# A Hymba encoder layer on Trainium2: every gate/up tile from 4 to 15 by seven block products, with the weight sums made by accumulating DMA

## The chip, the cores and the metric

The kernel runs on one core of a Trainium2 chip. The metric is the device time of one execution in microseconds. Before the change it is 1041.13 us, the median of 3 runs (1039.52 to 1042.09).

## The reference

One encoder layer over 16 meta tokens and 512 sequence tokens of width 1024. Its parts are a layer norm at the input, a SwiGLU network, a token mixer (windowed attention beside a gated linear attention), and a second SwiGLU network; a layer norm with a scaled residual follows each of the three. The change touches the first half of the two SwiGLU networks (f = 0 and f = 1):

```python
def swiglu(h, w_gate, w_up, w_down):
    return (jax.nn.silu(h @ w_gate) * (h @ w_up)) @ w_down
h = layer_norm(DN_ALPHA * h + 0.5 * swiglu(h, ffn1_w_gate, ffn1_w_up, ffn1_w_down), ffn1_ln_g, ffn1_ln_b)
```

Here h has 528 rows in the first network and 512 in the second (the meta tokens are dropped at the end), w_gate and w_up are 1024 x 2816, and w_down is 2816 x 1024. All inputs are float32.

## The kernel before

**Precision.** Each float32 operand is split into a high and a low half in f16, scaled by a power of two. A product then takes three matmuls: high by high, low by high, high by low. The scale of a weight chunk comes from a bound on its largest absolute value. ACT sums absolute values along each row (`weight_sum`, L1310) or DVE takes the row maximum (`chunk_max`, L1793); POOL reduces over the partitions (`over_all`, L2681); DVE makes the scale in four small instructions (`scale_of`, L1775 to L1780). Then ACT writes the high half (L1295, L1333 to L1336, L1344, L1349) and DVE the low half, in one SCALAR_TENSOR_TENSOR (L1815, L1873 to L1881, L1887, L1895).

**Tiles.** The 2816 hidden columns are 22 tiles of 128. Tile m needs 1024 x 128 columns of w_gate and of w_up: the weight chunk c = GU[f] + m, of 2048 float32 columns in 128 partitions (1024 KB), loaded by SP in two DMAs into one of two `stage` slots (L546, L547). SP loads chunk m as soon as the low half of chunk m - 2 is written (`w_ready`).

**Two ways to do a tile.** A plain tile takes 8 blocks of 128 rows for gate and 8 for up, three matmuls each, over all tokens: 96 matmuls of 264 columns in the first network, 48 of 512 in the second. A seven tile sees gate and up as a 2 x 2 block matrix (B11 and B21 the upper and lower half of gate, B12 and B22 those of up), and the tokens as a 2 x 2 one, and takes 7 block products in place of 8, as Strassen and Winograd do: 7 x 4 x 3 = 84 matmuls of 264 (256 in the second network) columns, `seven_product` (L682). It needs four sums of weight blocks, T1 to T4, and four sums of token blocks, S1 to S4 (made once for each network). DVE makes T1 to T4 in three instructions (`weight_sums`, L1860 to L1864), and combines the seven results with four additions (`product_sum`, L1908, L1912). Their order on PE is products 1, 6, 5, 7, then 2, 3, 4; products 2, 3 and 4 go on in banks that hold earlier products, so that product 2 waits until ACT has copied product 1 out (`p1_copy`, L1355), and products 3 and 4 wait for the second and third of DVE's additions (`seven_sum`).

**Order.** Before, tiles 4, 6, 8, 10, 12 and 14 are seven tiles and the tiles between them plain ones. PE does the first four products of tile m, the gate half of tile m + 1 (`gu_part`, L732), the last three products of tile m, and the up half of tile m + 1. Each engine's program is an order written out by hand in a loop over `SEVEN_AT`; semaphores tie them together. An engine that waits holds up all that stands behind it.

Of the kernel before, what the change touches and what calls it, by code (L numbers as in the profile page):

```python
# [24 lines left out]
F16 = mybir.dt.float16  # L25
# [93 lines left out]
B_STEPS = 9  # L119
# [6 lines left out]
def build(nc, x_in, meta_in, params, rel_in, head_in, ident_in, masks_in, reset_in, w2_in,  # L126
          gate, up, down, w_in, w_out, out):
    with ExitStack() as ctx:
# [132 lines left out]
        t_sum = part("arena", [P, 4, 4 * P])  # L261
        seven_w = part("arena", [P, 2 * N_PROD * 4 * P]).bitcast(F16).rearrange("p (b q i n) -> p b q i n", b=2, q=2, i=N_PROD)
# [137 lines left out]
        t_done = sem("t_done")  # L400
        seven_hi = sem("seven_hi")
        seven_ready = sem("seven_ready")
        gate_half_hi = sem("gate_half_hi")
        gate_half_ready = sem("gate_half_ready")
# [139 lines left out]
        def _(sp):  # L544
# [9 lines left out]

            for i in range(N_TOK):
                sp.dma_start(x_tok[:, i, :], x_in[i]).then_inc(x_loaded[i], 16)
                if i == 1:
                    load_gu(0, 0, 0)
            load_gu(0, 1, 1)
            for f in range(2):  # L560
                for m in range(2):
                    if f:
                        sp.wait_ge(w_ready, GU[f] + m - 1)
                        load_gu(f, m, (GU[f] + m) % 2)
                with sp.Fori(0, (N_GU - 2) // 2) as i:
                    for t in range(2):
                        sp.wait_ge(w_ready, GU[f] + 1 + t + 2 * i)
                        load_gu(f, 2 * i + 2 + t, (GU[f] + t) % 2)
# [18 lines left out]
        def _(pe):  # L587
# [99 lines left out]
            def seven_first(f, m):  # L687
                g = seven(f, m)
# [26 lines left out]

            def gu_part(f, m, g):
                s = m % 2
                if g == 0:
                    pe.wait_ge(gate_half_ready, seven(f, m - 1) + 1)

                    pe.wait_ge(hid_done, KF * f + m + 1)
                else:
                    pe.wait_ge(w_ready, GU[f] + m + 1)
                for k in range(KD):
                    for wp, xp in PRODUCTS:
                        w = wsp[:, (GU[f] + m) % 2, wp, (g * KD + k) * P:(g * KD + k + 1) * P]
                        for h in [None] if f else range(2):
                            if h is None:
                                dst, x = acc(1, 4 * s + 2 * g), tokens(1, xs[:, xp, k, :])
                            else:  # L730
                                dst, x = acc_half(f, 4 * s + 2 * g, h), xs[:, xp, k, token_half(2 * f, h)]
                            mm = nc.tensor.matmul(dst, w, x, start=k == 0 and wp + xp == 0, stop=k == KD - 1 and xp == 1)  # L732
                mm.then_inc(gu_ready if g else gate_part, 1)
# [50 lines left out]
            def ffn(f):  # L784
# [15 lines left out]
                for m in range(PAIR_END, KF):  # L800
# [410 lines left out]
        def _(act):  # L1211
# [112 lines left out]
            def seven_split_hi(f, m):  # L1324
                c, g = GU[f] + m, seven(f, m)
                slot = c % 2
                scale = wscale[:, slot:slot + 1]
                w = seven_w[:, g % 2, 0, :, :]
                quarter = stage[:, slot, 0:GU_COLS].rearrange("p (q n) -> p q n", n=4 * P)
                act.wait_ge(w_scale, 4 * c + 3)  # L1330
                if g >= 2:
                    act.wait_ge(seven_done, N_PROD * (g - 1))
                nc.scalar.activation(w[:, B11:B21 + 1, :], quarter[:, 0:2, :], ACT.Copy, scale=scale).then_inc(seven_hi, 1)  # L1333
                nc.scalar.activation(w[:, B22, :], quarter[:, 3, :], ACT.Copy, scale=scale).then_inc(w_hi, 1)
                act.wait_ge(t_done, 3 * g + 3)
# [1447 lines left out]
```

## Time and profile before

| what | value |
|---|---|
| median of 3 runs | 1041.13 us (1039.52 to 1042.09) |
| the profiled execution: its time, its span | 1039.09 us, 1037.3 us |
| granted TensorE clock, mean | 0.988 |
| busy: PE, PEld, DVE, ACT, POOL | 970.1, 693.6, 760.3, 494.8, 52.1 us |
| tiles 4 to 15, first network | 73.22 to 196.38 us of the span |
| tiles 4 to 15, second network | 717.52 to 838.22 us of the span |

Durations of instructions are from this one execution. Matmuls are pipelined: one shows some 276 ns, but a group's start to the next group's start, divided by its matmuls, gives the rate at which PE takes them. A busy PE that is idle nowhere is therefore read from starts.

### The profile page before, as it was taken

To read this page: it belongs to the slowest core of one execution; us is meant where nothing else is said; L and a number is where in the kernel's file an instruction comes from. 1 tells how busy PE (TensorE), PEld (TensorE's weight loads), DVE (VectorE), ACT (ScalarE), POOL (GpSimd) and SP (SyncE) were. 2 spreads that over 40 slices of the span, in tenths; PEclk is the share of its full clock that TensorE was granted. 3 is DMA by queue.
4 is the path that set the end of the run, shared out by engine and by line. 5 is a ranking of instruction groups with operands and counts; after the bars stand their busy time and mean duration, and the time that the engine had idled before them with its cause. 6 is when DMAs were issued, how large, how long until landed. Compare 5 with 4: busy or idle time off the path is not lost.

```text
span 1037.3 us, 17455 instructions
## 1 busy us (share of the span) xinstructions
PE 970.1 (94%) x7131; PEld 693.6 (67%) x7131; DVE 760.3 (73%) x1344; ACT 494.8 (48%) x707; POOL 52.1 (5%) x96
## 2 busy tenths in 40 slices
PE   2999999999999999999997899899899999999995
PEld 1888888888788886875565437665566644434584
DVE  6877766577987676877567978878777667889634
ACT  5576655244422245763335752567666434342214
POOL 0000000000020000000000010001000000011000
PEclk9999999999999999999998989999999999999999
DMA  5233322233334300212111012122332322424002
GB/s 210 84 111 122 114 91 94 77 109 120 112 119 152 123 2 1 82 42 71 52 41 42 1 35 88 49 74 82 123 122 88 117 82 82 163 99 170 15 1 82
DMA packets 24993, 89.26 MB, mean 86 GB/s; under 512 B 3035, under 2 KB 5427, under 8 KB 24915
## 3 DMA queue, kind: packets, MB, share of 16 engines
q1 hardware_dynamic: 23904, 87.17, 24.6%
q8 instruction: 56, 0.92, 0.4%
q10 hardware_dynamic: 1011, 0.99, 0.3%
q14 instruction: 22, 0.18, 0.1%
HBM read 86.05 MB, written 2.10 MB: 85 GB/s over the span
## 4 chain that ended last, share of the span: by engine, by line
PE 57%; DVE 25%; ACT 10%; issue 5%; DMA 2%; POOL 1%; SPq 0%; ACTq 0%; DVEq 0%
PE PS L732 9%; PE PS L682 9%; PE PS L758 8%; PE PS L853 7%; PE PS L652 6%; DVE cmax L1793 5%; PE PS L760 4%; DVE wsp L1815 4%; PE PS L763 3%; ACT wsp L1295 2%; PE PS L827 1%; DVE big L2020 1%; ACT H L1289 1%; PE PS L1133 1%; PE PS L976 1%
## 5 line engine op out<-in xcount | busy, mean ns | idle before, releaser
L652 PE MATMUL PS<-xs,wsp 128*128 128x264 f16 (+1 forms) x1344 | 195.4, 307 | 5.6 <-DVE wsp L1815 4.5
L652 PEld LDWEIGHTS PS<-xs,wsp 128*128 128x128 f16 x1344 | 131.0, 98 | 68.9 <-DVE wsp L1815 7.9
L732 PE MATMUL PS<-xs,wsp 128*128 128x264 f16 (+1 forms) x864 | 130.9, 310 | 0.0
L1793 DVE TENSOR_REDUCE cmax<-stage 128x1 f32<-128x2048 f32 (+2 forms) x47 | 120.2, 2557 | 4.5 <-DMA stage<-in_w_out 3.6
L1295 ACT ACTIVATE wsp<-stage,wscale 128x2048 f16<-128x2048 f32 (+2 forms) x34 | 70.8, 2081 | 100.0 <-DVE wscale L1779 78.1
L732 PEld LDWEIGHTS PS<-xs,wsp 128*128 128x128 f16 x864 | 84.5, 98 | 39.9
L2681 POOL PARTITION_ALL_REDUCE call<-cmax x73 | 48.8, 669 | 894.8 <-DVE cmax L1793 652.4
L1815 DVE SCALAR_TENSOR_TENSOR wsp<-stage,wscale,wsp 128x2048 f16<-128x2048 f32 (+2 forms) x34 | 83.3, 2449 | 12.8 <-ACT wsp L1295 12.8
L758 PE MATMUL PS<-big,arena 128*128 128x264 f16 (+1 forms) x792 | 89.4, 274 | 0.0
L758 PEld LDWEIGHTS PS<-big,arena 128*128 128x128 f16 x792 | 77.5, 98 | 11.5
L763 PE MATMUL PS<-big,wsp 128*128 128x264 f16 x660 | 75.1, 276 | 1.4 <-DVE big L2020 1.3
L760 PE MATMUL PS<-big,wsp 128*128 128x512 f16 x330 | 72.1, 379 | 2.5 <-DVE big L2020 1.7
L763 PEld LDWEIGHTS PS<-big,wsp 128*128 128x128 f16 x660 | 64.1, 98 | 12.2 <-issue 1.5
L682 PE MATMUL PS<-X,arena 128*128 128x264 f16 (+1 forms) x576 | 67.8, 274 | 0.0
L853 PE MATMUL PS<-xs,wsp 128*128 128x264 f16 (+1 forms) x384 | 67.3, 328 | 0.0
L682 PEld LDWEIGHTS PS<-X,arena 128*128 128x128 f16 x576 | 56.3, 98 | 7.5
L760 PEld LDWEIGHTS PS<-big,wsp 128*128 128x128 f16 x330 | 31.7, 98 | 42.9 <-issue 2.8
L682 PE MATMUL PS<-xs,arena 128*128 128x264 f16 (+1 forms) x432 | 53.7, 274 | 5.0 <-DVE big L1918 3.7
L853 PEld LDWEIGHTS PS<-xs,wsp 128*128 128x128 f16 x384 | 35.8, 98 | 24.2 <-issue 1.9
L682 PEld LDWEIGHTS PS<-xs,arena 128*128 128x128 f16 x432 | 42.0, 98 | 13.8 <-issue 6.3
L1310 ACT ACTIVATE big<-stage 128x2048 f16<-128x2048 f32 x26 | 49.3, 1897 | 2.8 <-DMA stage<-in_up 2.8
L1827 DVE SCALAR_TENSOR_TENSOR big<-PS,oscale,tmp_a 128x528 f32<-128x528 f32 (+1 forms) x32 | 24.2, 757 | 31.5 <-ACT tmp_a L1302 31.4
(267 smaller groups left out, 1421.8 us busy)
## 6 DMA issues: line engine op xcount, KB each, us to landing
stage<-in_gate SPq DMA_DIRECT2D x44, 512.0 KB, 3.7
stage<-in_up SPq DMA_DIRECT2D x44, 512.0 KB, 4.5
stage<-in_down SPq DMA_DIRECT2D x32, 704.0 KB, 5.3
stage<-in_w_in SPq DMA_DIRECT2D x16, 512.0 KB, 4.6
stage<-in_w_out SPq DMA_DIRECT2D x8, 512.0 KB, 4.2
X<-in_x SPq DMA_DIRECT2D x4, 512.0 KB, 6.2
out_T<-H SPq DMA_DIRECT2D x16, 128.0 KB, 1.7
stage<-in_w_in SPq DMA_DIRECT2D x2, 576.0 KB, 4.8
```

Source lines behind the costliest of these rows:

```text
L652: return nc.tensor.matmul(dst, w, x, start=k == 0 and wp + xp == 0, stop=k == KD - 1 and xp == 1)
L682: mm = nc.tensor.matmul(PS[:, 4 * (m % 2) + bank, 0:ln_width(2 * f)], seven_w[:, seven(f, m) % 2, wp, w, k * P:(k + 1) * P], seven_tokens( ...
L732: mm = nc.tensor.matmul(dst, w, x, start=k == 0 and wp + xp == 0, stop=k == KD - 1 and xp == 1)
L758: mm = nc.tensor.matmul(PS[:, bank, 0:ln_width(2 * f)], w, x[:, token_half(2 * f, h)], **flags)
L760: mm = nc.tensor.matmul(acc(1, bank), w, tokens(1, x), **flags)
L763: mm = nc.tensor.matmul(PS[:, bank + g, 0:HALF], w, x[:, token_half(0, g)], **flags)
L853: mm = nc.tensor.matmul(dst, x if lhs_is_x else w, w if lhs_is_x else x, start=k == 0 and wp + xp == 0, stop=k == KD - 1 and xp == 1)
L1295: nc.scalar.activation(wsp[:, slot, 0, 0:cols], stage[:, slot, 0:cols], ACT.Copy, scale=wscale[:, slot:slot + 1]).then_inc(w_hi, 1)
L1310: nc.scalar.activation(sum_out[:, :], stage[:, slot, 0:GU_COLS], ACT.Abs, accum_out=cmax[:, slot:slot + 1]).then_inc(w_sum, 1)
L1793: nc.vector.tensor_reduce(cmax[:, one], stage[:, slot, 0:cols], AX.X, ALU.max, apply_absolute_value=True).then_inc(w_max, 1)
L1815: nc.vector.scalar_tensor_tensor(wsp[:, slot, 1, 0:cols], stage[:, slot, 0:cols], wscale[:, one], wsp[:, slot, 0, 0:cols], ALU.mult, ALU.s ...
L2681: nc.gpsimd.partition_all_reduce(call[:, c % 2:c % 2 + 1], cmax[:, c % 2:c % 2 + 1], P, LARGEST).then_inc(w_all, 1)
```

## The change

All twelve tiles from 4 to 15 become seven tiles, and `gu_part` goes. The raw weights of a seven tile lie in one of three buffers (`raw`: the two `stage` slots and a new one in the arena), the split ones in three as well (one of them is the memory of `wsp`). The four weight sums are no longer made by DVE. SP loads, beside gate and up, a second copy of up and of the lower half of gate into `sums_at`, and POOL adds to these in place with five accumulating DMAs of 128 x 512 float32 (256 KB each), in two rounds. In the first round B12 becomes T1 = B12 + B11, and two of the copies become T3 = B12 + B22 and B21 + B22; in the second, T2 = B22 + T1 and T4 = B21 + B22 + T1. Since only additions are made, signs move into the token sums and into a negated scale (`up_scale`, `xinv_neg`). The bound of a seven tile is now the sum of absolute values over B11, B21, T1 and B22, so that it waits for the first round; the bounds of chunks 16 and 17 are ACT's too. On POOL the order for a tile is: three transfers, partition reduce, two transfers.

```diff
@@ constants
-SEVEN_AT = [4, 6, 8, 10, 12, 14]
+SEVEN_AT = list(range(4, 16))
-SUMMED_FROM = 3
-B11, B21, B22, T1, T3, T2, T4 = range(7)
+SEVEN_END = SEVEN_AT[-1] + 1
+SUMMED = range(3, 18)
+N_BUF = 3
+B11, B21, T1, B22, T3, T2, T4 = range(7)
+N_RAW = 4
@@ buffers
-        t_sum = part("arena", [P, 4, 4 * P])
-        seven_w = part("arena", [P, 2 * N_PROD * 4 * P]).bitcast(F16).rearrange("p (b q i n) -> p b q i n", b=2, q=2, i=N_PROD)
+        raw_third = part("arena", [P, GU_COLS])
+        seven_w = [part("arena", [P, N_PROD * 4 * P]).bitcast(F16) for _ in range(2)]
+        seven_w.insert(1, wsp[:, :, :, :].rearrange("p a b n -> p (a b n)")[:, 0:2 * N_PROD * 4 * P])
@@ helpers
+        def raw(f, m):
+            return raw_third if buf(m) == 0 else stage[:, f if buf(m) == 1 else 1 - f, 0:GU_COLS]
+        def sums_at(m):
+            row = 6 + 3 * (m - SEVEN_AT[0]) if m < SEVEN_AT[0] + N_BUF else 15 + 3 * buf(m)
+            return big[:, row * T:row * T + 3 * 4 * P]
@@ sync (SP)
+            def load_seven(f, m):
+                i = m - SEVEN_AT[0]
+                if i == 0:
+                    if f == 0:
+                        sp.wait_ge(tok_sq, N_TOK)
+                    else:
+                        sp.wait_ge(x_ready, ln_tile(2, 2 * KD))
+                elif i < N_BUF:
+                    sp.wait_ge(w_ready, GU[f] + i + 2)
+                else:
+                    sp.wait_ge(raw_ready, seven(f, m - N_BUF) + 1)
+                    sp.wait_ge(t_second, 16 * (seven(f, m - N_BUF) + 1))
+                    sp.wait_ge(t_third, 16 * (seven(f, m - N_BUF) + 1))
+                done = seven_loaded[buf(m)]
+                sp.dma_start(raw(f, m)[:, 0:KD * P], gate[f][m]).then_inc(done, 16)
+                sp.dma_start(raw(f, m)[:, KD * P:GU_COLS], up[f][m]).then_inc(done, 16)
+                if N_BUF <= i < 2 * N_BUF:
+                    sp.wait_ge(s_ready2, 4 * f + 4)
+                elif i >= 2 * N_BUF:
+                    sp.wait_ge(w_ready, GU[f] + m - N_BUF + 1)
+                sp.dma_start(sums_at(m)[:, 0:KD * P], up[f][m]).then_inc(done, 16)
+                sp.dma_start(sums_at(m)[:, KD * P:12 * P], gate[f][m][:, 4 * P:KD * P]).then_inc(done, 16)
+                for m in range(2, 4):
+                    if m == 3:
+                        load_seven(f, SEVEN_AT[0])
+                    sp.wait_ge(w_ready, GU[f] + m - 1)
+                    load_gu(f, m, (GU[f] + m) % 2)
+                for m in SEVEN_AT[1:]:
+                    load_seven(f, m)
+                for m in range(SEVEN_END, KF):
+                    if m < SEVEN_END + 2:
+                        sp.wait_ge(raw_ready, seven(f, m - 2) + 1)
+                        ...
+                    load_gu(f, m, (GU[f] + m) % 2)
@@ tensor (PE)
             def seven_first(f, m):
-                pe.wait_ge(w_ready, GU[f] + m + 1)
-                pe.wait_ge(seven_ready, 2 * g + 2)
+                pe.wait_ge(raw_ready, seven(f, m) + 1)
                 pe.wait_ge(hid_done, KF * f + m + 1)
                 seven_product(f, m, 0)
+                pe.wait_ge(w_ready, GU[f] + m + 1)
                 ...
                 for m in SEVEN_AT:
                     seven_first(f, m)
-                    gu_part(f, m + 1, 0)
                     seven_second(f, m)
-                    gu_part(f, m + 1, 1)
@@ scalar (ACT): weight_sum reads raw(f, m) after t_first in seven tiles
+            def raw_split_hi(f, m):
+                act.wait_ge(w_scale, 4 * c + 3)
+                act.wait_ge(t_first, 48 * (g + 1))
+                if m >= SEVEN_AT[0] + N_BUF:
+                    act.wait_ge(seven_done, N_PROD * (g - N_BUF + 1))
+                elif buf(m) == 1:
+                    act.wait_ge(gu_ready, classic(f, SEVEN_AT[0] - 1))
+                nc.scalar.activation(seven_w[buf(m)][:, 0, 0:N_RAW, :], blocks(raw(f, m)), ACT.Copy, ...).then_inc(raw_hi, 1)
+            def sums_split_hi(f, m):
+                act.wait_ge(t_second, 16 * (g + 1))
+                act.wait_ge(t_third, 16 * (g + 1))
+                nc.scalar.activation(seven_w[buf(m)][:, 0, N_RAW:N_PROD, :], blocks(sums_at(m)), ACT.Copy, ...).then_inc(w_hi, 1)
                 for m in SEVEN_AT:
+                    if m + 1 < SEVEN_END:
+                        raw_split_hi(f, m + 1)
+                    else:
+                        act.wait_ge(seven_done, N_PROD * (seven(f, m - 1) + 1))
+                        split_hi(GU[f] + m + 1, (GU[f] + m + 1) % 2, GU_COLS)
                     p1_copy(f, m)
+                    if m > SEVEN_AT[0]:
+                        seven_gate(f, m - 1, 1)
+                    if m + 1 < SEVEN_END:
+                        sums_split_hi(f, m + 1)
+                    if m + 3 in SUMMED:
+                        weight_sum(f, m + 3)
                     hidden_sum(f, m - 1)
                     seven_gate(f, m, 0)
@@ vector (DVE): weight_sums, seven_split_lo, gate_lo and up_lo go
+            def raw_split_lo(f, m):
+                dve.wait_ge(raw_hi, g + 1)
+                nc.vector.scalar_tensor_tensor(w[:, 1, 0:N_RAW, :], blocks(raw(f, m)), ...).then_inc(raw_ready, 1)
+            def sums_split_lo(f, m):
+                dve.wait_ge(w_hi, c + 1)
+                dve.wait_ge(raw_ready, g + 1)
+                nc.vector.scalar_tensor_tensor(w[:, 1, N_RAW:N_PROD, :], blocks(sums_at(m)), ...).then_inc(w_ready, 1)
                 for m in SEVEN_AT:
+                    if m > SEVEN_AT[0]:
+                        product_sum(f, m - 1, 3)
+                    scale_only(m + 2)
+                    if m + 1 < SEVEN_END:
+                        raw_split_lo(f, m + 1)
+                    else:
+                        chunk_lo(GU[f] + m + 1, (GU[f] + m + 1) % 2, GU_COLS)
+                    if m > SEVEN_AT[0]:
+                        seven_hidden(f, m - 1)
+                    out_scale_only(m + 1)
                     product_sum(f, m, 0)
                     product_sum(f, m, 1)
                     product_sum(f, m, 2)
+                    if m + 1 < SEVEN_END:
+                        sums_split_lo(f, m + 1)
@@ gpsimd (POOL)
+            def first_sums(f, m):
+                quarter = blocks(raw(f, m))
+                pool.wait_ge(seven_loaded[buf(m)], seven_loads(f, m))
+                pool.dma_start(quarter[:, T1, :], quarter[:, B11, :], accum_op=ALU.add).then_inc(t_first, 16)
+                pool.dma_start(blocks(sums_at(m))[:, T3 - N_RAW, :], quarter[:, B22, :], accum_op=ALU.add).then_inc(t_first, 16)
+                pool.dma_start(blocks(sums_at(m))[:, T4 - N_RAW, :], quarter[:, B22, :], accum_op=ALU.add).then_inc(t_first, 16)
+            def second_sum(f, m):
+                pool.wait_ge(t_first, 48 * (seven(f, m) + 1))
+                pool.dma_start(blocks(sums_at(m))[:, T2 - N_RAW, :], blocks(raw(f, m))[:, T1, :], accum_op=ALU.add).then_inc(t_second, 16)
+            def third_sum(f, m):
+                pool.wait_ge(t_first, 48 * (seven(f, m) + 1))
+                pool.dma_start(blocks(sums_at(m))[:, T4 - N_RAW, :], blocks(raw(f, m))[:, T1, :], accum_op=ALU.add).then_inc(t_third, 16)
                 for c in range(0 if f == 0 else OUT0 + 1, DN[f] + 2):
+                    m = c - GU[f]
+                    if m in SEVEN_AT:
+                        first_sums(f, m)
                     over_all(c)
+                    if m in SEVEN_AT:
+                        second_sum(f, m)
+                        third_sum(f, m)
```

## Rows read from the trace of the kernel before

**Rows 1.** The page's first part: busy time, share and instructions of each engine.

```profile
PE 970.1 (94%) x7131; PEld 693.6 (67%) x7131; DVE 760.3 (73%) x1344; ACT 494.8 (48%) x707; POOL 52.1 (5%) x96
```

**Rows 2.** Windows over tiles 4 to 15, both networks; last columns clock, DMA share, GB/s.

```profile
73.22:196.38 123.16, 121.83 (x1083) 105.51 (x1080) 83.35 (x141) 72.65 (x98) 5.74 (x11) 1.00 0.30 98
717.52:838.22 120.70, 117.50 (x792) 77.24 (x793) 83.94 (x142) 72.15 (x98) 5.82 (x12) 1.00 0.30 103
```

**Rows 3.** Timeline of PE, first network: start, duration, instructions, idle before and its releaser.

```profile
78.62 5.56 PE L732 MATMUL PS<-xs,wsp 128*128 128x264 f16 x48
84.02 1.51 PE L682 MATMUL PS<-xs,arena 128*128 128x264 f16 x12
...
94.67 1.51 PE L682 MATMUL PS<-xs,arena 128*128 128x264 f16 x12 [1.03 <-DVE big L1918]
...
114.91 0.28 PE L682 MATMUL PS<-xs,arena 128*128 128x264 f16 x1
```

**Rows 4.** The same timeline in the second network.

```profile
717.52 1.47 PE L682 MATMUL PS<-xs,arena 128*128 128x256 f16 x12 [1.24 <-issue]
...
739.91 1.47 PE L682 MATMUL PS<-xs,arena 128*128 128x256 f16 x12 [2.70 <-DVE big L1918]
...
759.44 1.47 PE L682 MATMUL PS<-xs,arena 128*128 128x256 f16 x12
```

**Rows 5.** Page, DMA issues: kilobytes each, median us from issue to landing.

```profile
stage<-in_gate SPq DMA_DIRECT2D x44, 512.0 KB, 3.7
stage<-in_up SPq DMA_DIRECT2D x44, 512.0 KB, 4.5
...
out_T<-H SPq DMA_DIRECT2D x16, 128.0 KB, 1.7
```

**Rows 6.** Timeline of POOL, two stretches of the first network.

```profile
70.23 1.99 POOL L2681 PARTITION_ALL_REDUCE call<-cmax  x1 [12.84 <-ACT big L1310]
...
88.81 0.61 POOL L2681 PARTITION_ALL_REDUCE call<-cmax  x1 [8.83 <-ACT big L1310]
```

**Rows 7.** Timeline of DVE in the same two stretches.

```profile
69.67 2.34 DVE L1881 SCALAR_TENSOR_TENSOR arena<-arena,wscale 128x2048 f16<-128x2048 f32 x1
...
93.75 0.77 DVE L1918 SCALAR_TENSOR_TENSOR big<-tmp_b,oscale,tmp_a 128x528 f32<-128x528 f32 x1 [0.65 <-ACT tmp_a L1366]
94.56 0.16 DVE L1821 TENSOR_TENSOR oscale<-winv,xinv 128x1 f32<-128x1 f32 x1
...
99.47 1.21 DVE L1860 TENSOR_TENSOR arena<-stage 128x1024 f32<-128x1024 f32 x1
...
102.55 0.89 DVE L1912 TENSOR_TENSOR tmp_b<-PS,tmp_b 128x264 f32<-128x264 f32 x2
103.79 1.28 DVE L1873 SCALAR_TENSOR_TENSOR arena<-stage,wscale,arena 128x1024 f16<-128x1024 f32 x1 [0.35 <-ACT arena L1333]
...
106.29 2.35 DVE L1881 SCALAR_TENSOR_TENSOR arena<-arena,wscale 128x2048 f16<-128x2048 f32 x1 [0.34 <-ACT arena L1336]
```

**Rows 8.** Timeline of ACT, first network.

```profile
91.07 0.46 ACT L1366 ACTIVATE tmp_a<-PS,oscale 128x264 f32<-128x264 f32 x1
...
96.82 1.90 ACT L1310 ACTIVATE big<-stage 128x2048 f16<-128x2048 f32 x1
98.62 0.19 ACT L1310 ACTIVATION_READ_ACCUMULATOR big<-stage 128x1 f32 x1
...
98.98 0.63 ACT L1316 ACTIVATE arena<-big 128x528 f16<-128x528 f32 x1
...
104.27 1.99 ACT L1336 ACTIVATE arena<-arena,wscale 128x2048 f16<-128x2048 f32 x1
```

**Rows 9.** Timeline of SP's DMA issues ahead of the second network's tile 4.

```profile
672.19 0.34 SPq L546 DMA_DIRECT2D stage<-in_gate  x1
```

**Rows 10.** Timeline of DVE at that place: the last split of the tokens.

```profile
689.10 0.48 DVE L1760 SCALAR_TENSOR_TENSOR xs<-H,xscale,xs 128x256 f16<-128x256 f32 x1 [0.50 <-ACT H L1289]
```

**Rows 11.** Page, DMA queues: packets, MB, share of 16 engines.

```profile
q1 hardware_dynamic: 23904, 87.17, 24.6%
```

More of the change, by code:

```diff
@@ L118 @@
 LATE_STEPS = 2 * NORM_STEPS + 2
-B_STEPS = 9
+B_STEPS = 10
 def slopes():
@@ L155, in build @@
         oscale = sb("oscale", [P, 2])
+        up_scale = sb("up_scale", [P, 2])
+        xinv_neg = sb("xinv_neg", [P, 3])
         oscale_b = sb("oscale_b", [P, 2])
@@ L399, in build @@
         w_sum = sem("w_sum")
[L400 to L404, printed above, removed]
+        seven_loaded = [sem(f"seven_loaded{i}") for i in range(N_BUF)]
+        t_first = sem("t_first")
+        t_second = sem("t_second")
+        t_third = sem("t_third")
+        raw_hi = sem("raw_hi")
+        raw_ready = sem("raw_ready")
         s_added = sem("s_added")
@@ L521, in summed @@
         def summed(c):
-            return any(GU[f] + SUMMED_FROM <= c < GU[f] + PAIR_END for f in range(2))
+            return any(c - GU[f] in SUMMED for f in range(2))
         def sums_through(c):
@@ L531, in maxima_through, with loads_through, seven_loads, buf @@
             return c + 1 - sums_through(c)
+        def loads_through(c):
+            return 32 * sum(all(i - GU[f] not in SEVEN_AT for f in range(2)) for i in range(c % 2, c + 1, 2))
+        def seven_loads(f, m):
+            return 64 * (N_SEVEN // N_BUF * f + (m - SEVEN_AT[0]) // N_BUF + 1)
+        def buf(m):
+            return (m - SEVEN_AT[0]) % N_BUF
+        def raw(f, m):
[3 more added lines that the diff above has]
+            return big[:, row * T:row * T + 3 * 4 * P]
+        def blocks(ap):
+            return ap.rearrange("p (i n) -> p i n", n=4 * P)
         def by_half(f, ap):
@@ L560, in _ @@
             for f in range(2):
-                for m in range(2):
-                    if f:
+                if f:
+                    for m in range(2):
                         sp.wait_ge(w_ready, GU[f] + m - 1)
                         load_gu(f, m, (GU[f] + m) % 2)
[L565 to L568, printed above, removed]
+                for m in range(2, 4):
[8 more added lines that the diff above has]
+                        sp.wait_ge(raw_ready, seven(f, m - 2) + 1)
+                        sp.wait_ge(t_second, 16 * (seven(f, m - 2) + 1))
+                        sp.wait_ge(t_third, 16 * (seven(f, m - 2) + 1))
+                    else:
+                        sp.wait_ge(w_ready, GU[f] + m - 1)
+                    load_gu(f, m, (GU[f] + m) % 2)
                 for n, q in enumerate(DN_ORDER):
@@ L714, in seven_second @@
                 seven_product(f, m, 6)
[L716 to L733, printed above, removed]
             def down_tile(f, q, h=None, between=None):
@@ new lines, in raw_split_hi @@
+                if m >= SEVEN_AT[0] + N_BUF:
+                    act.wait_ge(seven_done, N_PROD * (g - N_BUF + 1))
+                elif buf(m) == 1:
+                    act.wait_ge(gu_ready, classic(f, SEVEN_AT[0] - 1))
+                nc.scalar.activation(seven_w[buf(m)][:, 0, 0:N_RAW, :], blocks(raw(f, m)), ACT.Copy,
+                                     scale=wscale[:, c % 2:c % 2 + 1]).then_inc(raw_hi, 1)
+            def sums_split_hi(f, m):
+                c, g = GU[f] + m, seven(f, m)
+                act.wait_ge(t_second, 16 * (g + 1))
+                act.wait_ge(t_third, 16 * (g + 1))
+                nc.scalar.activation(seven_w[buf(m)][:, 0, N_RAW:N_PROD, :], blocks(sums_at(m)), ACT.Copy,
+                                     scale=wscale[:, c % 2:c % 2 + 1]).then_inc(w_hi, 1)
@@ L1884, in gate_lo @@
[L1884 to L1896 removed]
+                w = seven_w[buf(m)]
```

191 lines of the change are left out of this document (59 added, 132 removed).

## The prediction

> **What bounds the kernel now.** I read the page's busy shares first: PE is busy 94% of the span, the next engine 73% [rows 1]. An average hides stages, so I read the two stretches that the change touches, tiles 4 to 15 of each network, 123.16 and 120.70 us. PE is busy 121.83 and 117.50 us of them at clock 1.00, DVE and ACT some 84 and 72, POOL under 6, and the DMA engines 30% [rows 2]. The timeline of PE shows the stage's rhythm: 48 matmuls from 78.62 to 84.02, so 5.40/48 = 0.1125 us for one of 264 columns, and no gap from one pair of tiles to the next, 94.67 to 114.91, 20.24 us [rows 3]. In the second network a pair takes 759.44 - 739.91 = 19.53 us [rows 4]. Its only gaps are at the start: 1.03 us in the first network [rows 3], 1.24 and 2.70 in the second [rows 4]. So the stage is PE's; all that surrounds it now fits under 20 us for two tiles. The question is whether it fits under two of the new, shorter tiles.
>
> **PE.** A seven tile is 84 matmuls: 84 x 0.1125 = 9.45 us. In the second network a pair is 84 matmuls of 256 columns and 48 of 512, which count as 96 of 256: 84/180 x 19.53 = 9.11 us. Twelve tiles without a gap are 113.4 and 109.4 us, 9.8 and 11.3 less than now. So 21 us is the most that the change can give.
>
> **What leaves other engines.** DVE loses three additions for each old seven tile (1.21 us for 1024 columns, L1860, and two of half that width). It gains one tiny multiply a tile (like L1821, 0.16) [rows 7]. Per tile it then does a raw split 2.35, a sums split of 1536 columns (between 1.28 and 2.35: 1.8), four scale instructions (0.6), two output scales (0.3), four sums (2.0) and the hidden tile 0.77 [rows 7]: 7.8 us. ACT does 1.99 + 1.5 for the splits, 2.1 for the sum of absolutes, 0.8 for the hidden sum and 1.4 for the copy and two silus [rows 8]: 7.8 us. Both fit in 9.11. Sign changes and the added `xinv_neg` cost nothing beside the matmuls of tiles 2 and 3. So no engine's busy time is the bound; the order of waits is.
>
> **DMA and POOL.** SP loads 1792 KB a tile in place of 1024. A 512 KB load lands after 3.7 us; the second, issued some 0.4 later, 4.5 after its own issue, so 1024 KB land after 4.9 [rows 5]: 1.2 us for each further 512 KB. The trace has no transfer issued by POOL and none that accumulates, so two costs are unknown.
> - *Issue on POOL.* Lower end: 0.34 us, SP's issue of a plain DMA [rows 9]. Upper end: 1.99 us, POOL's reduce at 70.23, which ran beside a two-input DVE instruction (69.67 to 72.01); it takes 0.61 at 88.81 [rows 6, 7]. I take 0.61, the row of the same engine undisturbed.
> - *First round, R* (three issues to the last landing, 768 KB). Lower end: three short issues (1.0) and the landing of 256 KB, between the 1.7 of a 128 KB store and 3.7 [rows 5]: 2.4, together 3.4. Upper end: 3 x 1.99 + 2.4 = 8.4. An accumulating transfer needs the target's old bytes besides the source's; 1536 KB land after 3.7 + 2 x 1.2 = 6.1. I take 6.1, also because the next tile's loads are under way on the same 16 engines.
>
> **The loop that sets the pace.** From tile 10 on, the third and fourth load of tile m wait for `w_ready` of tile m - 3, because they overwrite its sums. From there every step waits for the one before:
> loads (768 KB) 4.3; first round R; sum of absolutes 1.90 + 0.19; then, as ACT is in order, hidden sum 0.8, silu 0.46 and only then the raw split of tile m - 1, 1.99 [rows 8]; DVE's raw split 2.35, and, in order behind it, hidden tile 0.77, output scales 0.3, three sums 1.3, sums split 1.8 [rows 7]. The last is `w_ready` of tile m - 1: the loop turns once for two tiles. Without R it is 4.3 + 2.1 + 0.8 + 0.46 + 1.99 + 2.35 + 0.77 + 0.3 + 1.3 + 1.8 = 16.2 us; with R = 6.1, 22.3, so 11.1 us a tile against PE's 9.45. With R = 3.4 it is 9.8. PE sees it as late products 3 and 4, since the raw split stands ahead of the sums in DVE's order. Tiles 5 to 9 have the shorter form (raw buffer free after the raw split); I give them the same pace, since they inherit the late start.
> POOL's own loop is shorter: two issues 1.2, R 6.1, sum 2.1, reduce 0.61 = 10.0 us.
>
> **Starts and ends.** First network, tile 4: ACT must sum chunk 6 before the raw split of tile 5 and `p1_copy`. The reduce of chunk 5 ends at 72.2 [rows 6]; two issues bring 73.4, the round 79.5, the sum 81.6, the split 83.6, the copy 84.0. Product 7 ends at 73.22 + 4 x 1.35 = 78.6: PE waits 5.4 us, and 1.9 more because DVE's raw split (to 86) precedes its sums. Tile 4 takes 9.45 + 7.3, 16.8 us. Second network: SP now puts tile 4's loads, which wait for the last token split (689.10 + 0.48) [rows 10], ahead of chunk 3's, issued at 672.19 so far [rows 9]. That lands near 699, and its sum, reduce, scale and splits put tile 3 some 2.5 us late and tile 4 1.3 later than now; tile 4 itself takes 16.5. At the ends, chunks 16 and 17 reuse buffers only two tiles back, and ACT's sum of them waits for their landing; I get 11.7 and 12.6 us for tiles 14 and 15 whatever R is, hidden in the pace at R = 6.1.
>
> **Sum.** First network: 16.8 + 11 x 11.1 = 139 us against 123.2: +16. Second: 1.3 + 16.5 + 122 = 140 against 120.7: +19. The profiled execution took 1039.09 us, its span 1037.3, and would take 1074; it lies 2.0 under the median of the three runs, 1041.13, and on that scale I say 1076 us.
>
> **A rule that speaks against the change.** The Trainium skill, *Collectives: The Full Stack*, "The bandwidth ceiling: the fold count and why AG ≠ RS ≠ AR", says that a reducing DMA reads two sources for each byte written, both through the same read ring, and so moves at half a copy's rate. No run here shows an accumulating transfer. By it R is at least the 6.1 above and the DMA engines' own time becomes a rival, below; by a copy's price R would be 4.3 (3.7 and half of 1.2) and the time 1061.
> A second rule, *SBUF — State Buffer*, "Who interferes with whom", says that a two-input DVE instruction blocks GpSimd's reads, and (inferred there) not the writing of descriptors. The trace agrees with its first half (1.99 against 0.61) [rows 6]; by the second half no issue would be held.
>
> **Rivals.**
> - *PE stays dense* (faster). If the loads and R take under 18.9 - 11.9 = 7.0 us together (6.3 in the second network), the loop hides and PE's order decides: 21 us less, 1020; with some stall at the starts up to 1036. For it: the DMA engines are 70% idle now [rows 2]. Against: even the lowest ends make 4.3 + 3.4 = 7.7.
> - *Cheap transfers, but waits at both ends.* R = 3.4: tile 4 takes 2.7 less than above, nine tiles 9.8 each, the last two 11.7 and 12.6: 126.6 and 127.6 us, so +3 and +7, 1051.
> - *The DMA engines are the bound.* The queue moved 87.17 MB in 24.6% of 16 engines' span, 342 GB/s [rows 11]. A tile's 1792 KB and 1280 KB counted twice are 4.46 MB, 13.0 us. 24 x 13.0 = 313 against 243.9: 1111.
> - *POOL is the bound.* Issues of 1.99 us, each held as the reduce was: 2 x 1.99 + 8.4 + 2.1 + 2.0 = 16.5 us a tile, 1193. POOL's loop passes the one above from an issue of some 1.1 us on. For it is the held reduce of rows 6; against it their other row, and that every issue would have to be held.
> - *No change*: the gain of PE and the stalls cancel, 1038 to 1044.
>
> **How the numbers follow.** The loop as worked out, pace 10.2 to 12 us, 1058 to 1100: 0.46. DMA-bound 0.17, cheap 0.11, POOL 0.06: with these, slower 0.80. Dense PE, or nearly: 0.15 faster. Within 0.3% (some 3 us, what a measurement of this kernel can tell): 0.05. The range leaves out most of the dense case below and the POOL case with the worst of the DMA case above: 1032 to 1130.
>
> **What would show it.** Right: in the windows of rows 2, stages longer than now; PE waiting inside seven tiles for DVE's sums (tmp_b) and ACT's copy, at most tiles; ACT's sum of absolutes waiting for a DMA; the first round near 6 us; a POOL issue under 1.2 us. Wrong: starts of tiles 9.45 us apart with no gap (then my loop has slack that I don't see), a first round under 3 us, or DMA engines over 90% busy, which is the DMA rival. The gap at product 2 of tile 4 should be there in either case.

## The result and the profile after

The changed kernel takes 1161.03 us, the median of 4 runs (1155.65 to 1163.55), beside 1041.61 (1039.52 to 1043.08) for the kernel before on the same chip: 1.1141 times as long, 95% interval 1.1096 to 1.1186. The direction was foreseen; the time lies 85 us over the 1076 forecast and 31 over the top of the range. The profiled run took 1163.55 us, its span 1161.7.

The page's busy row and, further down, its queues and transfers (columns as in [rows 1, 5, 11]):

```profile
PE 1000.4 (86%) x7275; PEld 722.2 (62%) x7275; DVE 760.7 (65%) x1365; ACT 518.6 (45%) x727; POOL 148.1 (13%) x216
...
q1 hardware_dynamic: 30816, 106.05, 25.7%
q0 software_dynamic: 17280, 31.46, 16.7%
...
big<-stage POOLq DMA_DIRECT2D x64, 256.0 KB, 5.3
```

Two prices that the trace before could not give stand here. q0 holds the accumulating transfers: 31.46 MB in 16.7% of 1161.7 us is 162 GB/s, 1.62 us of all 16 engines for one of 256 KB. q1, the loads, runs at 355 GB/s (106.05 MB in 25.7%). A tile thus needs 5 x 1.62 = 8.1 us for its sums and 5.2 for its loads: 13.3 us of the DMA engines.

The stages, answering [rows 2], and below them tiles 6 to 13 of the first network alone:

```profile
76.00:252.49 176.49, 129.71 (x1008) 102.95 (x1009) 91.09 (x160) 85.26 (x110) 49.20 (x65) 0.89 0.78 190
787.08:962.52 175.44, 135.20 (x1009) 107.41 (x1009) 90.36 (x160) 84.24 (x110) 50.01 (x65) 0.85 0.79 191
...
119.67:226.46 106.79, 83.21 (x673) 67.35 (x672) 59.40 (x104) 55.38 (x72) 34.53 (x45) 0.94 0.89 211
```

The stages grew by 53.3 and 54.7 us; the span by 124.4. The rest, by the starts in PE's timelines: tile 4 comes 2.8 us later in the first network, tiles 2 and 3 of the second take 9.0 more (787.08 - 755.94 against 717.52 - 695.39), and 4.4 lie between the stages, behind tile 21 of the first network, in a stretch that the change does not touch; their cause stays open.

One turn of the steady state, while PE is at tile 11, from the timeline of POOL, and ACT's sum in it:

```profile
191.60 0.34 POOL L2694 PARTITION_ALL_REDUCE call<-cmax  x1 [8.99 <-ACT big L1362]
191.82 0.89 POOL L2707 DMA_DIRECT2D big<-arena  x1
192.38 1.22 POOL L2712 DMA_DIRECT2D big<-arena  x1
193.22 1.27 POOL L2700 DMA_DIRECT2D stage<-stage  x1
193.76 1.62 POOL L2701 DMA_DIRECT2D big<-stage  x1
194.30 1.97 POOL L2702 DMA_DIRECT2D big<-stage  x1
205.34 0.34 POOL L2694 PARTITION_ALL_REDUCE call<-cmax  x1 [9.08 <-ACT big L1362]
```

```profile
203.24 1.91 ACT L1362 ACTIVATE big<-stage 128x2048 f16<-128x2048 f32 x1 [6.71 <-DMA big<-stage]
```

From one reduce to the next are 13.7 us: POOL issues the second round of a tile (L2707, L2712) and the first of the next (L2700 to L2702) some 0.54 us apart, and then stands until ACT has summed what that round brought. The one longer step, 0.84 us ahead of 193.22, is a wait for the loads: SP issued them from 187.09 on, and by the trace the last landed at 192.94. The first round takes 193.22 to 203.24, 10.0 us; in the queue it stands behind the second round of the tile before: the five transfers land at 195.22, 196.73, 198.25, 200.66 and 203.22, one after the other.

PE at tiles 4 and 5, the timeline that [rows 3] show of before, and below it what POOL and ACT did in the gap:

```profile
76.00 1.52 PE L749 MATMUL PS<-xs,arena 128*128 128x264 f16 x12 [2.07 <-DVE arena L1901]
...
94.95 2.82 PE L749 MATMUL PS<-xs,arena 128*128 128x264 f16 x12 [11.00 <-ACT tmp_b L1399]
...
110.55 2.82 PE L749 MATMUL PS<-xs,wsp 128*128 128x264 f16 x12 [3.67 <-ACT tmp_b L1399]
114.42 2.82 PE L749 MATMUL PS<-X,wsp 128*128 128x264 f16 x12 [1.04 <-DVE tmp_b L1926]
117.03 2.81 PE L749 MATMUL PS<-xs,wsp 128*128 128x264 f16 x12
```

```profile
76.97 0.35 POOL L2694 PARTITION_ALL_REDUCE call<-cmax  x1 [7.27 <-ACT big L1362]
...
78.28 1.57 POOL L2700 DMA_DIRECT2D stage<-stage  x1
...
90.73 1.91 ACT L1362 ACTIVATE big<-stage 128x2048 f16<-128x2048 f32 x1 [11.82 <-DMA big<-stage]
```

Besides the gap of 11.00 us, note the durations: after the waits twelve matmuls take 2.82 us in place of 1.52, at the lower of the clock's two levels (1.2 of 2.4 GHz). The window over the last three groups shows the granted clock, third number from the end (the DMA share behind it is rough in so short a window):

```profile
110.55:119.67 9.12, 8.08 (x36) 5.28 (x37) 5.90 (x8) 2.70 (x3) 1.54 (x2) 0.50 1.06 237
```

The four such groups shown cost at most 4 x 1.3 = 5.2 us more.

PE's waits (engine, line, what it waited for: us in total, times, longest):

```profile
PE PS L749 <- DVE tmp_b L1926: 46.7, 24, 2.4
...
PE PS L749 <- ACT tmp_b L1399: 37.2, 15, 11.0
```

Every seven tile waits for DVE's sums, 15 for ACT's copy.

### The profile page after: what moved, and what is told of

The parts are those of the page before. It is cut to its first block and busy times, and to the rows that moved or that the text cites. A ratio compares the mean times of both kernels' runs of the same rounds, so it can differ in the third digit from the quotient of the medians.

```text
span 1161.7 us, 17889 instructions
## 1 busy us (share of the span) xinstructions
PE 1000.4 (86%) x7275; PEld 722.2 (62%) x7275; DVE 760.7 (65%) x1365; ACT 518.6 (45%) x727; POOL 148.1 (13%) x216
## 3 DMA queue, kind: packets, MB, share of 16 engines
q1 hardware_dynamic: 30816, 106.05, 25.7%
q0 software_dynamic: 17280, 31.46, 16.7%
## 5 line engine op out<-in xcount | busy, mean ns | idle before, releaser
L719 PE MATMUL PS<-xs,wsp 128*128 128x264 f16 (+1 forms) x1344 | 197.1, 309 | 10.3 <-DVE wsp L1859 8.1
L719 PEld LDWEIGHTS PS<-xs,wsp 128*128 128x128 f16 x1344 | 131.5, 99 | 74.7 <-DVE wsp L1859 11.2
L749 PE MATMUL PS<-X,arena 128*128 128x264 f16 (+1 forms) x768 | 97.7, 287 | 33.8 <-DVE tmp_b L1926 30.7
L1837 DVE TENSOR_REDUCE cmax<-stage 128x1 f32<-128x2048 f32 (+2 forms) x43 | 111.1, 2584 | 4.0 <-DMA stage<-in_w_out 3.7
L749 PE MATMUL PS<-xs,arena 128*128 128x264 f16 (+1 forms) x576 | 85.9, 311 | 32.2 <-ACT tmp_b L1399 26.1
L749 PEld LDWEIGHTS PS<-X,arena 128*128 128x128 f16 x768 | 76.6, 102 | 51.7 <-DVE tmp_b L1926 34.1
L749 PEld LDWEIGHTS PS<-xs,arena 128*128 128x128 f16 x576 | 63.1, 111 | 50.5 <-ACT tmp_b L1399 28.9
L1819 DVE TENSOR_SCALAR cexp<-call 128x1 int32<-128x1 int32 x73 | 10.9, 150 | 91.6 <-POOL call L2694 91.6
L898 PE MATMUL PS<-xs,wsp 128*128 128x264 f16 (+1 forms) x384 | 67.3, 328 | 0.0
L749 PE MATMUL PS<-X,wsp 128*128 128x264 f16 (+1 forms) x384 | 49.3, 289 | 16.0 <-DVE tmp_b L1926 16.0
L749 PE MATMUL PS<-xs,wsp 128*128 128x264 f16 (+1 forms) x288 | 44.6, 316 | 11.0 <-ACT tmp_b L1399 11.0
L749 PEld LDWEIGHTS PS<-X,wsp 128*128 128x128 f16 x384 | 38.5, 102 | 24.9 <-DVE tmp_b L1926 18.7
```

The source lines that it names most:

```text
L719: return nc.tensor.matmul(dst, w, x, start=k == 0 and wp + xp == 0, stop=k == KD - 1 and xp == 1)
L898: mm = nc.tensor.matmul(dst, x if lhs_is_x else w, w if lhs_is_x else x, start=k == 0 and wp + xp == 0, stop=k == KD - 1 and xp == 1)
L1837: nc.vector.tensor_reduce(cmax[:, one], stage[:, slot, 0:cols], AX.X, ALU.max, apply_absolute_value=True).then_inc(w_max, 1)
```

## The experiments

The theories: D, the DMA engines, full (B in the first four texts); C, the chain of waits that the prediction named (A in the first four); P, the loop through POOL's order, which came up after these four. Stage times below are worked out from the starts of each tile's first matmul in the timelines of PE, as the mean of the two networks; "dense" is 84 matmuls a tile at the rates of [rows 3, 4]. Each ratio is to the kernel before on the chip where the variant ran; its medians there were 1041.6 us, 1044.7 (e1 to e4), 1043.0 (e5 to e8) and 1042.8 (e9, e10), so a difference between two variants of different chips can be some 3 us off. In e5 to e9 each of the semaphores `t_first`, `t_second` and `t_third` is also split into one for each buffer.

| kernel | median us (range) | ratio, 95% | tiles 4 and 5 | each of 6 to 13 | tiles 14 and 15 |
|---|---|---|---|---|---|
| dense PE | | | 18.6 | 9.3 | 18.6 |
| forecast | 1076 | | 27.8 | 11.1 | 22.2 |
| changed | 1161.0 (1155.7-1163.6) | 1.114 (1.110-1.119) | 43.3 | 13.3 | 26.0 |
| e1_reorder | 1125.5 (1124.1-1129.3) | 1.079 (1.075-1.082) | 33.7 | 13.4 | 18.7 |
| e2_plain | 1101.2 (1090.5-1105.2) | 1.053 (1.045-1.060) | 29.3 | 12.0 | 24.4 |
| e3_small_loads | 1155.4 (1152.0-1156.9) | 1.105 (1.102-1.109) | 43.0 | 13.2 | 26.0 |
| e4_tiny_sums | 1080.1 (1078.8-1081.2) | 1.034 (1.031-1.037) | 29.9 | 10.5 | 24.8 |
| e5_pool_order | 1176.9 (1170.2-1183.9) | 1.127 (1.120-1.134) | 38.2 | 14.7 | 24.4 |
| e6_pool_small | 1100.1 (1097.9-1104.5) | 1.055 (1.051-1.060) | 29.4 | 11.8 | 19.3 |
| e7_pool_swap | 1110.3 (1107.7-1117.1) | 1.063 (1.060-1.067) | 28.6 | 13.1 | 19.0 |
| e8_pool_swap_plain | 1051.6 (1048.0-1054.8) | 1.009 (1.006-1.011) | 26.0 | 10.0 | 18.7 |
| e9_three_adds | 1066.1 (1063.7-1070.4) | 1.023 (1.018-1.027) | 26.4 | 10.8 | 18.7 |
| e10_gpsimd_adds | 1250.7 (1249.5-1251.2) | 1.198 (1.193-1.202) | 48.8 | 19.0 | 20.2 |

**e1_reorder**

```diff
 # ACT, tile m
-raw_split_hi(f, m + 1)
 p1_copy(f, m)
 ...
-weight_sum(f, m + 3)
 hidden_sum(f, m - 1)
 seven_gate(f, m, 0)
+raw_split_hi(f, m + 2)
+weight_sum(f, m + 3)
 # ahead of the loop: raw_split_hi(f, 5) in place of weight_sum(f, 6), which goes behind tile 4's p1_copy
 # DVE: scale_only(m + 2) behind the three product sums
```

> ACT's raw split of tile m + 2 (and the hidden sum and silu of tile m) stand ahead of its sum of absolutes of tile m + 3, and DVE's scale behind the raw split; every transfer stays. Theory A, the chain of waits sets the pace: in the changed kernel the loop from 'sums split written' over loads (6.1 us), first round (10.0), sum, hidden sum, silu and the two raw splits turned once in 27.4 us for two tiles; reordered it spans three tiles (some 28 us), 9.4 us a tile, so the steady tiles fall from 13.65 to about PE's 9.5 and the time to about 1075 us. Theory B, the DMA engines are full: a tile's loads need 5.2 us of all 16 engines and its accumulating transfers 8.1 (31.46 MB in 16.7% of the span), so steady tiles stay at 13.3 us or more with a DMA share of 0.95, only the starts gain (the 11 us wait at tile 4): 1130 to 1150 us.

The starts win 9.6 us and the ends 7.3 in each network, and tiles 14 and 15 are dense. The steady tiles don't move: 13.4 us. Tiles 6 to 13 of the first network, with the engines' share next to last:

```profile
109.50:215.50 106.00, 86.81 (x674) 68.05 (x672) 58.63 (x104) 57.16 (x73) 34.70 (x45) 0.90 0.91 213
```

So C sets the ends and part of the starts, and undoing it alone does not change the pace. The time lies 5 us under B's range, which had no gain at the ends.

**e2_plain**

```diff
-pool.dma_start(quarter[:, T1, :], quarter[:, B11, :], accum_op=ALU.add)
+pool.dma_start(quarter[:, T1, :], quarter[:, B11, :])   # and the other four
```

> The five transfers of a tile become plain copies of the same bytes from the same queue (the additions are left out). Theory B1, adding is what is dear, because the target must be read as well: the copies run at the loads' 350 GB/s, 3.7 us of all engines a tile in place of 8.1; DMA needs 8.9 us, the first round falls from 10 to about 5 us, the pace to about 10.6 and the time to about 1090 us. Rival C, it is POOL's way of issuing (its queue and its descriptors), not the adding: the queue stays at some 160 GB/s and the time at 1161.

The page's queue row of this kernel (span 1098.5 us):

```profile
q0 software_dynamic: 9600, 31.46, 7.5%
```

The same bytes take 7.5% in place of 16.7%: 382 GB/s against 162. Adding more than halves the rate, and 60 us go with it. The row shows one more difference: 9600 packets in place of 17280, since the copies go in packets of 4096 bytes and the adding transfers in 2048. That smaller packets are the cause is a rival, and the packets' times in the traces speak against it: in the changed kernel a packet of the loading queue takes 159 ns for 4096 bytes and 84 for 2048 (medians), one of 2048 added takes 187, and one of 4096 copied here 164. Halving the packet costs some 6%, adding more than doubles it.

The pace, 12.0, is above the 10.6 of the text, and the first round takes 4.4 to 8.0 us (four rounds from 145 to 187 us). Every second tile is dense, 9.45 us, and tiles 8, 10 and 12 of the first network take 14.7 to 17.4. Once for two tiles POOL stands waiting for loads:

```profile
145.25 0.54 POOL L2700 DMA_DIRECT2D stage<-stage  x1 [4.51 <-DMA big<-in_gate]
...
156.44 0.54 POOL L2700 DMA_DIRECT2D arena<-arena  x1
...
170.86 0.54 POOL L2700 DMA_DIRECT2D stage<-stage  x1 [4.68 <-DMA big<-in_gate]
```

That is the rhythm of C, one turn for two tiles: with the price of adding gone, the prediction's chain shows. e8, which undoes C's and P's orders, has 10.0; no run undoes C's alone there.

**e3_small_loads**

```diff
-sp.dma_start(sums_at(m)[:, 0:KD * P], up[f][m])
+sp.dma_start(sums_at(m)[:, 0:16], up[f][m][:, 0:16])   # from tile 10; gate's second copy too
```

> From tile 10 on the second copies of up and gate are loaded in 16 columns only (768 KB a tile taken away, every wait kept; the sums are not the true ones). Theory B: a tile needs 3.0 + 8.1 us of the DMA engines; while these loads would run (tiles 7 to 12) the pace falls from 13.6 to about 11.1, some 15 us for each network: about 1130 us. Theory A: only the load term of the loop falls, 6.1 to some 3 us in two tiles: pace 12.1, about 1140 us.

A miss for both theories: tiles 7 to 12, during which these loads run, stay at 13.2 to 13.8 us, though the engines need 11.1. Two stretches from one tile's start to the next, in windows (last columns clock, DMA share, GB/s), and the timelines of POOL and ACT:

```profile
158.04:171.66 13.62, 9.80 (x86) 8.05 (x84) 7.42 (x13) 7.04 (x9) 4.67 (x6) 1.00 0.83 178
171.66:185.18 13.52, 9.80 (x87) 8.05 (x84) 7.43 (x13) 7.04 (x9) 4.67 (x6) 1.00 0.83 173
```

```profile
161.96 0.35 POOL L2695 PARTITION_ALL_REDUCE call<-cmax  x1 [8.95 <-ACT big L1363]
162.18 0.89 POOL L2708 DMA_DIRECT2D big<-stage  x1
...
164.36 2.28 POOL L2703 DMA_DIRECT2D big<-stage  x1
175.48 0.35 POOL L2695 PARTITION_ALL_REDUCE call<-cmax  x1 [8.85 <-ACT big L1363]
```

```profile
173.38 1.91 ACT L1363 ACTIVATE big<-stage 128x2048 f16<-128x2048 f32 x1 [6.48 <-DMA big<-stage]
```

With the engines 17% idle the turn on POOL is still 13.5 us. From the first issue (162.18) to ACT's sum at 173.38, which waited for the first round, are 11.2 us, as long as the engines' 8.1 + 3.0; then come ACT's sum, 2.1, and the reduce, in which no transfer of POOL's is under way. This is where theory P came from: two bounds of one length, the engines' 13.3 and POOL's 13.5.

**e4_tiny_sums**

```diff
-pool.dma_start(quarter[:, T1, :], quarter[:, B11, :], accum_op=ALU.add)
+pool.dma_start(quarter[:, T1, 0:16], quarter[:, B11, 0:16], accum_op=ALU.add)   # and the other four
```

> The five accumulating transfers add 16 of 512 columns each (issues, waits and latencies stay, 97% of their bytes go; the sums are not the true ones). Theory B: DMA needs 5.3 us a tile; the first round falls to its fixed part, 3.5 to 4.5 us, the pace to 10.1 or PE's, the time to about 1080 us with the end waits (11 to 13 us for tiles 14 and 15) still there. If fixed costs (issue on POOL 0.54 us, latency) made the round long, the time stays above 1130.

As B has it: all waits and issues without the bytes, and 81 us are gone. The time is still 35 to 40 over before; what stays is 10.5 us a tile, the starts and both ends.

**e5_pool_order**

```diff
-if m in SEVEN_AT:
+if m == SEVEN_AT[0]:
     first_sums(f, m)
+if m in SEVEN_AT and m + 1 in SEVEN_AT:
+    first_sums(f, m + 1)
 over_all(c)
```

> The changed kernel with one edit: POOL issues the first round of tile m + 1 ahead of the partition reduce of tile m. Nothing else moves, every byte stays. Three theories of the 13.6 us a tile. P, POOL's loop: in one turn POOL issues the second round of m, the first round of m + 1, and then waits for ACT's sum of m + 1, which needs that round; the five transfers and the sum stand in one row (reduce at 191.60, next reduce at 205.34, 13.7 us). D, the DMA engines: 8.1 us for the accumulating and 5.2 for the loading queue, 13.3 us. C, the chain that the prediction named: 11.1 us or more. With this edit the loop of P is cut. P and D together: 13.3 us from the DMA engines, so little is won, 1145 to 1160 us, with a better start of tile 4. If P alone is the bound and the engines have room, 11 to 12 us a tile: 1100 to 1120.

A miss: slower than the changed kernel. POOL's timeline:

```profile
181.31 0.86 POOL L2698 DMA_DIRECT2D arena<-arena  x1 [10.15 <-DMA big<-in_gate]
181.84 1.21 POOL L2699 DMA_DIRECT2D big<-arena  x1
182.38 1.56 POOL L2700 DMA_DIRECT2D big<-arena  x1
182.96 1.32 POOL L2692 PARTITION_ALL_REDUCE call<-cmax  x1
...
196.77 0.86 POOL L2698 DMA_DIRECT2D stage<-stage  x1 [10.83 <-DMA big<-in_gate]
```

POOL is in order, and now waits for the loads of m + 1 ahead of the reduce of m. Those loads wait (through the splits of an older tile, which need the scale that follows the last reduce) for the reduce before: one wait was traded for another, 15.5 us a turn here.

**e6_pool_small**: e1's, e3's and e5's edits together.

> Three edits together: POOL's order as in e5_pool_order, ACT's and DVE's order as in e1_reorder, and the small second copies of e3_small_loads (from tile 10 of each network on, 16 columns in place of 1536, so that T2, T3 and T4 are sums of other numbers). With the small copies alone a tile stayed at 13.6 us while the DMA engines were 83% busy. P: the loop on POOL held it; now it is cut, and tiles 10 to 15 fall to what the DMA engines need, 8.1 + 3.0 = 11.1 us, so 12 tiles win 2.5 us over e1_reorder (1125), and the starts some more: 1085 to 1098. Q, the five accumulating transfers need 13.6 us for themselves, whatever stands around them: 13.6 us still, 1115 to 1125.

Between the two theories: tiles 10 to 13 take 12.1 us (the mean of the two networks), not 11.1, and not 13.6. The same orders with all bytes (e7) need 13.7 there. So with POOL's loop cut the bytes count, which they did not in e3. C's order is undone here too, and no run undoes P's alone with a gain (e5 traded its wait for another), so what P is worth by itself is argued from e3 and this run, not measured.

**e7_pool_swap**: e1's and e5's edits, and

```diff
-if m == 3:
+if m == 3 and f == 0:
     load_seven(f, SEVEN_AT[0])
 sp.wait_ge(w_ready, GU[f] + m - 1)
 load_gu(f, m, (GU[f] + m) % 2)
+if m == 3 and f == 1:
+    load_seven(f, SEVEN_AT[0])
```

> All bytes, POOL's order as in e5_pool_order, ACT's and DVE's as in e1_reorder, and in the second network SP issues the loads of tile 4 behind those of chunk 3, not ahead. D: the DMA engines are now all that is left, 13.3 us a tile: the first network's start wins some 5 us (first round of tile 6 done before ACT needs it), the second's start the same and the 4 to 8 us by which tiles 3 and 4 came late: 1100 to 1115. If the engines were not the bound in e1_reorder but POOL's loop alone, the tiles fall under 12 us: 1065 to 1085.

As D has it. In three windows, tiles 8 to 10 of the first network, the DMA engines have next to no idle time (over tiles 6 to 13 they are 0.94 busy, in the second network 0.91):

```profile
130.20:144.30 14.10, 11.29 (x86) 8.97 (x85) 7.33 (x13) 7.25 (x9) 6.04 (x9) 0.88 0.99 239
144.30:157.50 13.20, 10.06 (x87) 8.05 (x86) 7.33 (x13) 7.25 (x9) 4.59 (x8) 1.00 0.99 245
157.50:169.80 12.30, 9.95 (x86) 7.96 (x85) 7.33 (x13) 7.26 (x9) 4.01 (x8) 1.00 1.00 230
```

The orders are worth 51 us: 14.7 of them at each start, 7 at each end, little in the steady tiles. e5's edit, a loss by itself, is a small gain beside e1's: in the first network, where the third edit does nothing, the stage ends at 230.49 against e1's 234.41 (one profiled execution of each).

**e8_pool_swap_plain**: e7 with e2's edit.

> As e7_pool_swap, but the five transfers copy and don't add (the sums are then wrong numbers), with the same bytes and issues. The DMA engines then need 3.4 + 5.2 = 8.6 us a tile, less than PE's 9.45 and 9.11. If the bound is what adding costs on the DMA engines and the orders on POOL, ACT and SP, then all of it is gone here: PE is dense but for the starts of tile 4, 1022 to 1045, at or below the kernel before. If PE still waits in every tile, some other step is left that we have not named: above 1060.

Adding is worth 59 us of what e7 had left. Above the forecast all the same, and 0.9% above the kernel before. Tiles 6 to 13 of the first network:

```profile
102.40:182.80 80.40, 76.97 (x675) 65.08 (x673) 58.79 (x104) 57.32 (x73) 21.79 (x45) 1.00 0.83 287
```

That is 4.8 us over dense PE (8 x 9.45). The span is 10.4 us over before: each start (tiles 4 and 5) is 7.4 over dense PE, and each tile 4 comes some 3 us late besides; that eats what the twelve shorter tiles give.

**e9_three_adds**

```diff
-pool.dma_start(blocks(sums_at(m))[:, T4 - N_RAW, :], quarter[:, B22, :], accum_op=ALU.add)
+pool.dma_start(blocks(sums_at(m))[:, T4 - N_RAW, 0:16], quarter[:, B22, 0:16], accum_op=ALU.add)   # the second round's too
```

> As e7_pool_swap, but the two transfers that make T4 add 16 columns of 512 (T4 is then no sum; every issue, wait and load stays). In e7_pool_swap the DMA engines were 99 to 100% busy from 130 to 170 us at 12.3 to 14.1 us a tile. D, the DMA engines' time sets the pace: 3 x 1.62 + 5.2 = 10.1 us of it a tile in place of 13.3, 3.2 less; most of 22 tiles win 2 to 3 us, the first two little: 1050 to 1068, between e7_pool_swap (1110) and the kernel whose transfers only copy (1052). If it is the number of transfers, their issues or the rounds' waiting that costs, and not bytes added, this stays near 1100.

The queue's row (span 1061.8 us):

```profile
q0 software_dynamic: 17280, 19.28, 11.3%
```

As D has it: with all issues and rounds kept, the bytes of two of five transfers take 44 us, and the pace follows them: 13.1, 10.8, 10.0 us in e7, e9 and e8, where the rates above give 13.3, 10.1 and 8.6 us of DMA time (and dense PE 9.3).

**e10_gpsimd_adds**

```diff
-pool.dma_start(quarter[:, T1, :], quarter[:, B11, :], accum_op=ALU.add)
+nc.gpsimd.tensor_tensor(quarter[:, T1, :], quarter[:, T1, :], quarter[:, B11, :], ALU.add)   # T3, T2 and T4 likewise
```

> The four sums made by GpSimd's own tensor_tensor instructions in place of accumulating transfers: T3 = B12 + B22, T1 = B12 + B11, T2 = T1 + B22, T4 = T2 + B21, 128 x 512 each; no second copies are loaded, so a tile's loads are 1024 KB, 3.0 us of the DMA engines. POOL does the four in a row and then the partition reduce; ACT, DVE and SP order as in e7_pool_swap. If the DMA engines were all that kept the twelve tiles from PE's 9.45 us, PE is dense here but for the starts. A row that prices an add on GpSimd does not exist yet; if one takes under 1.5 us, POOL's loop (four adds, 0.35, ACT's sum 2.1 partly beside them) is under 8 us and the time is 1025 to 1050. Rival: DVE's two-input instructions hold POOL's adds, as they held a reduce for 1.99 us in the kernel before; with 4.9 us of such instructions a tile, the adds take over 9.5 us together and the tiles 11 to 14: 1080 to 1130.

Both theories missed. POOL's timeline:

```profile
178.45 1.27 POOL L2715 TENSOR_TENSOR big<-big,arena 128x512 f32<-128x512 f32 x1
185.92 0.38 POOL L2692 PARTITION_ALL_REDUCE call<-cmax  x1 [6.21 <-issue]
193.55 1.25 POOL L2703 TENSOR_TENSOR big<-stage 128x512 f32<-128x512 f32 x1 [7.25 <-issue]
194.94 1.26 POOL L2705 TENSOR_TENSOR stage<-stage 128x512 f32<-128x512 f32 x1
```

An add takes 1.26 us (92 of the 96; four at the starts took 2.0 to 2.2), but POOL stands some 6 us ahead of each reduce and 7 ahead of each first add, and nothing that the profile shows is waited for. Four adds (5.5, starts 1.4 apart), two gaps (5.95 and 7.25 on average) and the reduce (0.38) make the 19.0 us a tile. No kernel here beats the one before; by e8 the starts would have to be mended even if the transfers only copied.

## Why the prediction was wrong

- **The step that failed is the size of R.** "I take 6.1", upper end 8.4; the first round takes 10.0 us in the steady tiles and 12.4 at tile 4 (first issue 78.28, landed by ACT's sum at 90.73). I priced its three transfers as if they were alone. They stand in one queue behind the second round's two, each at 162 GB/s, and share the engines with 1792 KB of loads. The loads' term, 4.3, is short for the same reason: 187.09 to 192.94, 5.9 us. With R = 10.0 alone the prediction's own sum gives (16.2 + 10.0)/2 = 13.1 us a tile; 13.3 were measured.
- **POOL's loop, "10.0 us",** is 13.7 with that R. It was set aside as the shorter loop. It, the DMA engines and the chain that I took for the pace are of one length here: the chain turns in 27.4 us for two tiles (187.09 to 214.47, the end of the sums split), so it was real but not alone. e1 undid its order and the pace stayed; it shows once the adding is cheap, in e2. What all three share is the price of the adding bytes, and the pace falls with these (e2, e4, e9).
- **The rival "DMA engines are the bound", chance 0.17,** names what binds the steady tiles in the end: 13.0 us worked out, 13.3 needed, 13.3 measured. Its sign, engines over 0.90 busy, is met in part: 0.97, 0.87 and 0.97 in tiles 9 to 11 by their windows, 0.89 over tiles 6 to 13. That the tile takes just what the engines need is partly luck: e3 takes 13.2 us with engines that need 11.1, since POOL's loop is as long. The copy-twice price was right; the mistake was to hold a loop with an assumed transfer time for likelier than a count of bytes. Its 1111 (its terms give some 1110) had no starts or ends.
- **Starts: mechanism right, size too small.** Product 2 of tile 4 waited as described, but 11.0 us, not 5.4: ACT's sum of chunk 5 waited for its round, so that the reduce ended at 77.3, not 72.2, and then came R. A wait of 2.2 us for the sums split at product 6 was not in the sum. Tile 5, for which I took the pace, took 18.4 us, since it inherits the same lateness. The lower clock after each gap, at most 5 us of this, was not in the sum. Tiles 4 and 5 are 15.6 us over the forecast in each network, tiles 6 to 13 17.8 and the ends 3.8.
- **The second network's load order: right, undersized.** PE waits 4.4 us for tile 3 (2.5 said) and 4.0 more for tile 4, and with a lower clock in tile 3 (0.86 granted) tile 4 comes 9.0 us later than before (1.3 said).
- **Right:** the ends (11.7 and 12.6 us said, 26.0 together measured, gone in e1); the waits, 24 for DVE's sums and 15 for ACT's copy, and ACT's sum waiting for a DMA; a POOL issue, 0.54 us for 0.61, so that the rival "POOL is the bound", with issues of 1.99, did not come about; the engines' busy time, DVE 59.40 us in eight tiles, 7.4 each.
- **The Trainium skill's rule** from *Collectives: The Full Stack*, "The bandwidth ceiling: the fold count and why AG ≠ RS ≠ AR", that a reducing DMA moves at half a copy's rate, holds here and falls short, if anything: the plain copy's rate over the adding one's is 382/162 = 2.4 by the queues, 187/84 = 2.2 by packets of one size. I used it for R's floor and for a rival; the sum should have counted its price over all the bytes of a tile.

## What to carry to other kernels

Work moved from an engine to DMA is priced first as bytes over the engines' rate for that kind of transfer, all queues added up, and the loops of waits come after: here 13.3 us against 9.45. A transfer's time in a loop is that of all that stands ahead of it in its queue: here 10.0 us where I had priced 6.1. Issuing something earlier on an in-order engine helps only if what it waits for is there earlier too (e5).

## What was not expected of the hardware

- An accumulating transfer inside SBUF ran at 162 to 174 GB/s (e7: 31.46 MB in 16.2% of 1115.3 us), plain copies of the same blocks at 382 (e2).
- Changing between `tensor_tensor` and the partition reduce cost POOL 5.95 us on the way there (142.7 us in 24 waits) and 7.25 on the way back (174.1 in 24). The trace has 48 instructions MODIFY_POOL_CONFIG on the line of the first add and 48 on the reduce's, two for each change either way; the changed kernel has two in all. The Trainium skill, *GPSIMD Engine Reference*, "2.1 Instruction dispatch", says that the first call of a newly loaded GpSimd routine pays some 6 us; the trace agrees for the reduce. That loading is what fills both gaps was not tested apart.
